# Attention values of a two-layer encoder: each query tile in its own half of the TensorE array's columns

## The reference

```python
# A: latent attention (head width 96), B: grouped-query with axial rotary, both dense
s = jnp.einsum('bqgrd,bkgd->bgrqk', qblk, k) * scale
p = jax.nn.softmax(s, axis=-1)
o = jnp.einsum('bgrqk,bkgd->bqgrd', p, v)
# D: window of +-128 tokens with a sink logit per head
# C: three dilated sliding windows per head, merged by their softmax denominators
alpha = jax.nn.softmax(jnp.stack(lses, axis=0), axis=0)
o_c = jnp.einsum('gbsh,gbshd->bshd', alpha, outs)
# every branch output is projected, gated by a sigmoid and summed
merged = merged + gates[:, :, n] * (o.reshape(bsz, seq, 256) @ w_branch[n])
```

## Time and profile before

| what | value |
|---|---|
| time, median of 3 runs | 2089.31 us (2087.97 to 2090.29) |
| time of the profiled execution | 2088.28 us |
| its span in the profile | 2086.5 us |
| TensorE busy | 96% of the span |
| VectorE, ScalarE, GpSimd busy | 65%, 52%, 3% |
| mean granted TensorE clock | 0.984 |

### The profile page before, as it was taken

The page is one execution under the profiler, slowest core; times in us unless marked ns, Lnnn a source line. Parts: engine busy times, 40 slices in busy tenths (PEclk is TensorE's granted clock), DMA queues, the critical chain, the costliest instruction groups (busy, mean ns, idle before and its releaser), DMA issues.

```text
span 2086.5 us, 26833 instructions
## 1 busy us (share of the span) xinstructions
PE 2006.0 (96%) x9934; PEld 1681.0 (81%) x9934; DVE 1355.6 (65%) x1504; ACT 1094.9 (52%) x1126; POOL 57.5 (3%) x104
## 2 busy tenths in 40 slices
PE   7999998999998999999799999999999999999986
PEld 6888787999996878888688888888888888888864
DVE  3345335555546424435588988889888888888864
ACT  4232324333325332223477777777777777777743
POOL 2100002000002100000000000000000000000000
PEclk9999998999999999999799999999999999999998
DMA  8533335555535533323599999999989999998970
GB/s 297 162 101 101 101 104 184 182 181 183 188 132 214 191 105 118 101 82 120 207 344 345 350 374 339 362 342 354 374 321 374 345 355 348 350 374 325 373 287 23
DMA packets 253342, 506.66 MB, mean 243 GB/s; under 512 B 8304, under 2 KB 90384, under 8 KB 253152
## 3 DMA queue, kind: packets, MB, share of 16 engines
q1 hardware_dynamic: 250592, 497.92, 66.6%
q0 software_dynamic: 2688, 7.91, 1.3%
HBM read 504.75 MB, written 1.05 MB: 242 GB/s over the span
## 4 chain that ended last, share of the span: by engine, by line
PE 90%; DVE 4%; ACT 3%; issue 2%; DMA 1%; POOL 0%; DVEq 0%; SPq 0%; ACTq 0%; POOLq 0%
PE ps L1022 27%; PE ps L964 19%; PE ps L1168 11%; PE ps L934 9%; PE ps L866 4%; PE ps L1109 4%; PE ps L844 3%; PE ps L1175 3%; PE ps L1152 2%; PE ps L909 2%; PE ps L974 1%; PE ps L983 1%; PE ps L1140 1%; ACT down_hi_w L1371 1%; PE ps L1003 1%
## 5 line engine op out<-in xcount | busy, mean ns | idle before, releaser
L1803 DVE TENSOR_TENSOR ring_lo<-ring,up_gate_hi_w 128x2048 fp32r<-128x2048 f32 x224 | 504.3, 2288 | 59.5 <-ACT up_gate_hi_w L1368 58.5
L1368 ACT CAST up_gate_hi_w<-ring 128x2048 fp32r<-128x2048 f32 x224 | 423.1, 1914 | 84.4 <-DMA ring<-in_moe_w_up_dram 81.1
L1022 PE MATMUL ps<-up_gate_hi_w,tokens_hi 128*128 128x512 f32 x896 | 355.9, 397 | 1.3 <-DVE ring_lo L1803 1.3
L1022 PE MATMUL ps<-up_gate_hi_w,tokens_lo 128*128 128x512 f32 x896 | 350.0, 391 | 0.0
L1022 PE MATMUL ps<-ring_lo,tokens_hi 128*128 128x512 f32 x896 | 349.7, 390 | 0.0
L1808 DVE TENSOR_TENSOR down_lo_w<-ring,down_hi_w 128x2048 fp32r<-128x2048 f32 x112 | 256.6, 2291 | 56.3 <-ACT down_hi_w L1371 55.9
L1168 PE MATMUL ps<-hT,ring 128*128 128x256 f32 x1024 | 231.7, 379 | 0.0
L1371 ACT CAST down_hi_w<-ring 128x2048 fp32r<-128x2048 f32 x112 | 213.9, 1910 | 25.8 <-DMA ring<-in_moe_w_down_dram 24.9
L1168 PEld LDWEIGHTS ps<-hT,ring 128*128 128x128 f32 x1024 | 193.5, 190 | 26.5 <-issue 0.8
L1022 PEld LDWEIGHTS ps<-up_gate_hi_w,tokens_lo 128*128 128x128 f32 x896 | 168.6, 188 | 36.1
L1022 PEld LDWEIGHTS ps<-up_gate_hi_w,tokens_hi 128*128 128x128 f32 x896 | 168.6, 188 | 35.6 <-issue 1.7
(11 more groups left out here) (218 smaller groups left out, 2671.6 us busy)
## 6 DMA issues: line engine op xcount, KB each, us to landing
ring<-in_moe_w_up_dram SPq DMA_DIRECT2D x112, 1024.0 KB, 5.0
ring<-in_moe_w_gate_dram SPq DMA_DIRECT2D x112, 1024.0 KB, 5.1
ring<-in_moe_w_down_dram SPq DMA_DIRECT2D x112, 1024.0 KB, 8.4
ring<-in_w_in_dram SPq DMA_DIRECT2D x58, 1024.0 KB, 5.2
ring<-in_ffn_w_up_dram SPq DMA_DIRECT2D x16, 1024.0 KB, 5.4
ring<-in_ffn_w_gate_dram SPq DMA_DIRECT2D x16, 1024.0 KB, 8.0
ring<-in_ffn_w_down_dram SPq DMA_DIRECT2D x16, 1024.0 KB, 9.7
ring<-in_w_branch_dram SPq DMA_DIRECT2D x8, 1024.0 KB, 5.0
```

Of the source, the lines that this page charges most:

```text
L1022: m = mm(bank, xs[:, 4 * half + k, :], w[:, k, :], start=(half == k == n == 0), stop=(half == 1 and k == 3 and n == 2))
L1368: copy(up_gate_hi_w[:, j, :], ring[:, slot, :]).then_inc(run.up_gate_hi, 1)
L1803: v.tensor_tensor(ring_lo[:, slot, :], ring[:, slot, :], up_gate_hi_w[:, j, :], ALU.subtract)\
```

## The change

The output bank is now seen as two halves of 128 columns (`h`), one for the even and one for the odd head. Each product is split by query tile: tile 0 is computed in columns 0 to 63 of the array and lands in partitions 0 to 63, tile 1 in columns 64 to 127 and partitions 64 to 127. Both load the same block of values, each into its own half, and stream 128 columns instead of 256. The two halves take turns within a key tile. Nothing changes in the order of steps, in semaphores or in their counts.

Since a head's output now lies in both partition halves, the copy to `oT`, whose layout stays, is four instructions of 64x128, two of which move between partition halves. The last one updates `o_done`.

```diff
-        O_BANK = ps[:, 3, 0:SEQ]
+        O_BANK = ps[:, 3, 0:SEQ].rearrange("p (h s) -> p h s", h=2)
...
                             for kt in range(NT):
-                                m = mm(O_BANK[(h % 2) * HD:(h % 2 + 1) * HD, :], values(b, h, g, kt), pT[:, n % NPT, kt, :],
-                                       start=(g == 0 and kt == 0), stop=(g == NSETS[b] - 1 and kt == NT - 1))
+                                for t in range(NT):
+                                    m = mm(O_BANK[t * HD:(t + 1) * HD, h % 2, :], values(b, h, g, kt),
+                                           pT[:, n % NPT, kt, t * P:(t + 1) * P],
+                                           start=(g == 0 and kt == 0), stop=(g == NSETS[b] - 1 and kt == NT - 1))
...
-                        copy(oT[:, 2 * BRANCH_ID[b] + h // 2, :], O_BANK).then_inc(o_done, 1)
+                        for hh in range(2):
+                            for t in range(NT):
+                                ins = copy(oT[hh * HD:(hh + 1) * HD, 2 * BRANCH_ID[b] + h // 2, t * P:(t + 1) * P],
+                                           O_BANK[t * HD:(t + 1) * HD, hh, :])
+                        ins.then_inc(o_done, 1)
```

## The result

The changed kernel takes **2069.06 us** (median of 4 runs, 2068.25 to 2069.66) against 2089.80 us for the kernel before (4 runs, 2087.97 to 2091.49): a ratio of **0.9897, 95% interval 0.9885 to 0.9910**. It is 1% faster, 20.7 us, and beats the range's lower end (2070) by 0.9 us. The forecast was 2080.8, a gain of 8.5: the sign was right, the size was not.

What follows compares the result with a forecast made beforehand. TensorE, busy 96% of the span and carrying 90% of the chain, was taken to bound the kernel. 24 x 0.16 + 8 x 0.59 = 8.5 us off `pv`, copies nil, gave 2089.3 - 8.5 = 2080.8 us; range 2070 to 2099.

Steps and rivals of the forecast that it cites:

- `pv` time is passed on whole: Both attention stretches: TensorE bounds them, so what `pv` loses or gains there reaches the end whole, in both layers.
- The unit prices: TensorE in `pv`: 0.216 us per 256-column matmul, 0.109 per 128-column one, 0.053 for a group's opening load, 0.093 of drain.
- The copies are hidden: Output copies on ScalarE: four of 0.245 make 0.98 us, 9.9 us more in all, hidden; ScalarE or another lateness, chance 0.03.
- A shift of the clock: Granted clock at the stages' seams: low stretches may lengthen, go or come, 1.7 us either way, widening the range by 2.
- the middle case: `pv`: halves overlap with in-order issue, a product every 0.162 us, 0.85 and 2.15 us, gain 8.5 us; chance 0.38.
- The price that I put on a change of half: Inside `pv`: a 0.053 us load for the other half that nothing can hide, after each product's two matmuls.
- Full overlap: `pv`: the two halves run side by side, 0.69 and 1.56 us, gain 17.1 us, 2072.2 us; chance 0.20.
- The rivals on the slow side: `pv`: no overlap, 2089.7 us, chance 0.22; loads exposed without a drain, 2098.2, chance 0.10; with one, 2113, chance 0.07.
- exposed load: `pv`: a load exposed at all 160 changes of half, no overlap in return, +8.9 us, 2098.2 us; chance 0.10 without a drain.
- The bound on loads: `pv`, per set: eight loads of 0.053 make 0.42 us against four matmuls' 0.44, so the loads just permit side-by-side work.
- In turn: `pv`: two matmuls in one half, then a load for the other half, alternating, giving a product every 0.162 us.

Runs made afterwards that it cites:

- twice: The changed kernel with the four products of every set issued twice into the same sums: 2092.19 us, ratio 1.0007 to the kernel before.
- one_half: The kernel before with each product split by query tile, both tiles in the head's own column half, old single copy: 2089.95 us, ratio to before 0.9995.
- tiles_outer: The changed kernel with the loops over key tile and query tile exchanged, both key tiles of tile 0 first: 2070.77 us, ratio to before 0.9904.

## Why the prediction was wrong

**What held.** TensorE bounds both stretches and `pv` time is passed on whole: 20.3 us in `pv`, 20.2 in the two attention stretches, and `twice` gives back all it takes. The unit prices held: 0.216 and 0.109 a matmul, 0.053 for the opening load, 0.093 of drain (1.02 in `one_half`). The copies are hidden; each takes 0.26 and not 0.245, four of them 1.08 and not 0.98. A shift of the clock came, 1.4 us at the gather, and most of it was made up later.

**The step that failed** is the choice of the middle case, "halves overlap, but instructions leave the queue in order". Its 0.85 and 2.15 us for a `pv` measured 0.59 and 1.46. It rested on the earlier trace rows, where a load is issued as the matmul before it starts. In these rows all instructions are for one half, so that start can say when a load may go into its own half, and nothing of an instruction for the other. I read a limit of the half as a limit of the queue. `tiles_outer` shows it: the second half starts with the first, past three matmuls that are still waiting. The price that I put on a change of half, a 0.053 load that nothing hides, doesn't exist either, since loads for the two halves run together.

**A second error was in the bound itself.** Full overlap was worked out as 0.69 and 1.56, and so 17.1 us. The formula let a last product's two matmuls follow the steady rate of one product per 0.109, as if the second half began one matmul behind. Both halves begin together, and each has just four matmuls: 0.053 + 3 x 0.109 + 0.109 + 0.093 = 0.58; a C head has twelve, 1.45. The sum is 24 x 0.42 + 8 x 1.28 = 20.3. With it the rival "full overlap" would have read 2069.0, and the range, which takes 2 us off that case, would have begun at 2067, below the measured 2069.06. The Trainium skill, in "TensorE: Matmul & The Clock Gate", Part 3 ("Measured speedup vs the span model"), has about 4 ns from one tile's start to the next. The trace fits: the two first matmuls began within 0.01 us.

**The rivals on the slow side fell.** No exposed load: a change of half costs nothing (eight matmuls, three changes by program order, 0.59 us). The Trainium skill, in the same page's Part 3 ("The mechanism"), lets loads overlap running matmuls only in other row groups. The trace contradicts it between the halves too: both use all 128 rows, and their loads and matmuls ran together, eight of each in 0.59 us. The bound on loads, that eight of 0.053 just fit in 0.44, was no bound at all. `twice` also says so: its 16 loads reach over 0.85, and one behind the other they would need 15 x 0.053 + 0.137 = 0.93.

**"In turn" hardly matters** in this kernel: what matters is that the other half's work is within the queue's reach.

## What to carry to other kernels

A product whose stationary block is 64 columns wide leaves half the array idle. Splitting its moving columns over the two column halves took `pv` from 1.01 to 0.59 us and from 2.74 to 1.46 here, for float32 and full rows. Its price is to load the block twice, which cost no time. Keep the work of the two halves within four matmuls of each other in program order: with twelve, a C head took 2.38 us, which is seven tenths of its gain lost. And put such products next to each other: each pair saved 0.30 to 0.35 us of entering and leaving the half-width form. Work that is ready belongs in front of work that waits for a copy.

## What the runs showed that I had not expected

- Loads for the two halves run at the same time: 8 loads in 0.42 us, against 0.51 if one followed the other.
- The queue of TensorE reaches past instructions that wait for one half, so matmuls for different halves start out of program order. It did so past three matmuls that hadn't begun and not past four: blocks of 4, 8 and 12 matmuls per half gave C heads of 1.51, 1.94 and 2.38 us.
- Two float32 streams of 256 columns over all 128 rows, side by side, take as long as one (0.58 us for four matmuls).
- Stretches of half clock don't shift just as the work does: the gather of 32 matmuls took 6.65 us instead of 5.22 after everything had moved 19.8 us forward, and the stretch at 1040 to 1045 had no counterpart.
- Four ScalarE copies of 64x128 out of PSUM take 0.86 or 1.08 us, though each record is 0.26 in both.
